# Own input places for the third recurrence pair, four places for the attention gates, and another K order in six output tiles

## What is computed

```python
proj = h @ w_in                        # a_q, a_k, a_v, a_z, g_q, g_f, g_i, g_z: 8 parts of 1024 columns
att  = chunk_attention(a_q, a_k, a_v)  # 8 heads of 128, softmax over a band, relative bias
att  = att * silu(a_z)                 # the attention gates
hg   = hgrn2(g_q, g_f, g_i)            # 8 heads: q = silu(g_q), decay from sigmoid(g_f), a recurrence in chunks of 64
hg   = rms(hg) * silu(g_z)
x    = x + gate * (concatenate([att, hg]) @ w_out)
```

## Time and profile before

| what | value |
|---|---|
| median of the runs | 1596.85 us |
| span of the profiled execution | 1599.0 us |
| TensorE busy | 1573.0 us (98%) |
| VectorE busy | 1154.1 us (72%) |
| ScalarE busy | 862.4 us (54%) |
| DMA | 331 MB, mean 207 GB/s |
| mean granted TensorE clock | 0.994 of full speed |

### The profile page before, as it was taken

The page is one execution under the profiler, slowest core; times in us unless marked ns, Lnnn a source line. Parts: engine busy times, 40 slices in busy tenths (PEclk is TensorE's granted clock), DMA queues, the critical chain, the costliest instruction groups (busy, mean ns, idle before and its releaser), DMA issues.

```text
span 1599.0 us, 24289 instructions
## 1 busy us (share of the span) xinstructions
PE 1573.0 (98%) x9650; PEld 1400.7 (88%) x9650; DVE 1154.1 (72%) x1696; ACT 862.4 (54%) x1321; POOL 151.6 (9%) x164
## 2 busy tenths in 40 slices
PE   8998999989999999999999999999999999999999
PEld 6787889988999999988799888888888888888887
DVE  6797867877778886759778777777777777455544
ACT  6855546767665555655556454544444444444442
POOL 0000000321221220034213000000000000000000
PEclk9999999999999999999999999999999999999999
DMA  9999975533457774343244545555455454555552
GB/s 373 369 343 349 365 285 209 188 114 121 180 189 267 285 272 179 132 158 132 97 144 178 189 170 199 184 186 210 172 197 191 179 211 175 205 199 185 198 196 105
DMA packets 47825, 331.02 MB, mean 207 GB/s; under 512 B 5281, under 2 KB 6689, under 8 KB 8417
## 3 DMA queue, kind: packets, MB, share of 16 engines
q1 hardware_dynamic: 45184, 312.20, 53.5%
q0 software_dynamic: 2240, 17.04, 2.8%
q10 hardware_dynamic: 290, 0.25, 0.1%
HBM read 327.37 MB, written 2.10 MB: 206 GB/s over the span
## 4 chain that ended last, share of the span: by engine, by line
PE 89%; DVE 5%; DMA 3%; ACT 2%; issue 1%; POOL 0%; SPq 0%; ACTq 0%; DVEq 0%; POOLq 0%
PE ps L1173 20%; PE ps L1174 11%; PE ps L1169 9%; PE ps L1170 8%; PE ps L1171 8%; PE ps L1228 5%; PE ps L1227 5%; PE ps L1226 5%; PE ps L1216 4%; PE ps L1217 3%; PE ps L1218 3%; DVE wl L1916 2%; DMA raw<-in_wts 1%; DMA xs<-in_xN 1%; PE ps L1384 1%; PE ps L1351 1%
## 5 line engine op out<-in xcount | busy, mean ns | idle before, releaser
L1916 DVE TENSOR_TENSOR wl<-raw,wh 128x1024 fp32r<-128x1024 f32 x512 | 626.2, 1236 | 282.4 <-ACT wh L1519 281.9
L1519 ACT ACTIVATE wh<-raw 128x1024 fp32r<-128x1024 f32 x512 | 531.3, 1054 | 377.2 <-PE ps L1228 130.6
L1173 PE MATMUL ps<-hA,wh 128*128 128x512 f32 x1408 | 488.7, 390 | 0.0
L1174 PE MATMUL ps<-hA,wl 128*128 128x256 f32 x1408 | 397.0, 282 | 0.0
L1173 PEld LDWEIGHTS ps<-hA,wh 128*128 128x128 f32 x1408 | 264.2, 188 | 55.3
L1174 PEld LDWEIGHTS ps<-hA,wl 128*128 128x128 f32 x1408 | 266.1, 189 | 0.0
L1169 PE MATMUL ps<-hA,wh 128*128 128x256 f32 x752 | 219.5, 292 | 0.0
L1170 PE MATMUL ps<-hA,wh 128*128 128x256 f32 x752 | 211.7, 282 | 0.0
L1171 PE MATMUL ps<-hA,wl 128*128 128x256 f32 x752 | 211.7, 282 | 0.0
L1169 PE MATMUL ps<-hB,wh 128*128 128x256 f32 x576 | 164.4, 285 | 0.8 <-DVE work L2362 0.4
L1170 PE MATMUL ps<-hB,wh 128*128 128x256 f32 x576 | 161.1, 280 | 0.0
(11 more groups left out here) (303 smaller groups left out, 2077.9 us busy)
## 6 DMA issues: line engine op xcount, KB each, us to landing
raw<-in_wts SPq DMA_DIRECT2D x256, 1024.0 KB, 4.8
raw<-in_ada SPq DMA_DIRECT2D x36, 1024.0 KB, 6.1
side<-in_ada POOLq DMA_DIRECT2D x12, 1024.0 KB, 8.5
work<-in_memN SPq DMA_DIRECT2D x2, 1024.0 KB, 8.9
xs<-in_xN POOLq DMA_DIRECT2D x1, 2048.0 KB, 20.6
xs<-in_xT POOLq DMA_DIRECT2D x2, 1024.0 KB, 7.8
out_rows<-xs SPq DMA_DIRECT2D x8, 256.0 KB, 2.4
wp<-in_dt SPq DMA_DIRECT2D x8, 128.0 KB, 2.7
```

What stands on the lines that cost most here:

```text
L1173: e.matmul(ps[bank][:, :], w1, hl, start=first, stop=False)
L1174: i = e.matmul(ps[bank][:, T:2 * T], w2, hl[:, 0:T], start=False, stop=last)
L1519: e.activation(wh[:, h % WS, :], raw[:, n % RAW, part * HALF:(part + 1) * HALF], ACT.Copy).then_inc(s_hi)
L1916: e.tensor_tensor(wl[:, h % WS, :], src, wh[:, h % WS, :].bitcast(F32), ALU.subtract).then_inc(s_lo)
```

## The change

1. A tensor `third` of three places lies over K steps 12 to 14 of the tensor `hB2`. By `INPUT_SET = (1, 0, 2, 1)` pair 0 has the second place of f, q, z, pair 1 the first, pair 2 the places in `third`, pair 3 pair 0's. The calls `until(rt 0)` and `until(rt 1)` ahead of the tiles of pairs 2 and 3 become one, `until(rt 0)` ahead of those of pair 3. The head of the recurrence `rf` p now itself waits for `rt` p-2 (a new generator `rec_head`, and a semaphore wait of ScalarE ahead of the sigmoids), as kk and E still have two places.
2. The four gate tiles have a place each: the three that pair 1 used and one in `av`. So az0 now stands behind `until(rt 1)`, az3 behind attention heads 0 to 3, and the waits for `gate` n-2 are gone.
3. The first six tiles of the output product take their K in another order. `until` for heads 4 to 7, for gates 2 and 3, and the load of x stand ahead of its fifth half instead of its first. `rt` 3 is still asked for ahead of block 64; K steps 14 and 15 still begin at block 66.

```diff
+INPUT_SET = (1, 0, 2, 1)
 OUT_FIRST = 6
-OUT_PARTS = (tuple(range(8, 14)), (0, 2, 4, 6, 7), (14, 15), (1, 3, 5))
+OUT_STEPS = ((range(0, 4), (8, 9, 10, 11)), (range(0, 4), (0, 2)), (range(0, 4), (12, 13)), (range(4, 6), (8, 9, 10, 11, 12, 13, 0, 2)),
+             (range(0, 6), (4, 6, 7)), (range(0, 6), (14, 15)), (range(0, 6), (1, 3, 5)))
+    def rec_head(p):
+        while p >= 2 and ("rt", p - 2) not in o.done:
+            yield
+        yield from stages(("rf", p), REC_HEAD)
...
-        if kind != "az" and n >= 2:
-            o.until(("rt", n - 2))
+        if kind != "az" and n == 3:
+            o.until(("rt", 0))
         if kind == "az":
             if n == 0:
+                o.until(("rt", 1))
+            if n == 3:
                 o.until(*[("att", h) for h in range(4)])
-            if n >= 2:
-                o.until(("gate", n - 2))
...
-    o.until(*[("att", h) for h in range(4, 8)])
-    o.beat("xload", 0)
...
-    o.until(*[("rt", n) for n in range(3)])
-    o.until(*[("gate", m) for m in range(4)])
-    for i, h in enumerate(OUT_PARTS[1]):
-        o.add(i % 2, ("gs", h), stages(("gs", h), ("hi", "lo")))
+    def split_gates(*heads):
+        for lane, h in heads:
+            o.add(lane, ("gs", h), stages(("gs", h), ("hi", "lo")))
+
+    o.until(("rt", 0), ("rt", 1))
     for i in range(0, 16 * OUT_FIRST, 8):
+        if i == 8:
+            o.until(("gate", 0), ("gate", 1))
+            split_gates((5, 0), (5, 2))
+        if i == 16:
+            o.until(("gs", 0), ("gs", 2))
+        if i == 24:
+            o.until(("rt", 2))
         if i == 32:
-            o.until(*[("gs", h) for h in OUT_PARTS[1]])
+            o.until(*[("att", h) for h in range(4, 8)])
+            o.beat("xload", 0)
+            o.until(("gate", 2), ("gate", 3))
+            split_gates((0, 4), (1, 6), (0, 7))
+        if i == 48:
+            o.until(("gs", 4), ("gs", 6), ("gs", 7))
         if i == 64:
             o.until(("rt", 3))
...
                 if k == "sigmoid":
                     e.wait_ge(*after(("f", 2 * pr + 1), "act", "ev"))
+                    if pr >= 2:
+                        e.wait_ge(*after(("rt", pr - 2), "dve", "lo"))
...
-        zt = [av[:, 0, i, :] for i in range(2)]
+        zt = [fin2[:, 0, :], qin2[:, 0, :], zin2[:, 0, :], av[:, 0, 0, :]]
```

More of the change, by code:

```diff
@@ L142, in plan @@
             ada(2, gates.pop(0))
-    early, ends, late, last = [], [], [], []
     for j in range(KT):
@@ L146, in plan @@
             ada(2, gates.pop(0))
-        t = s_tile("w_out", (128 * j,))
-        if j < OUT_FIRST:
-            early.append([t[kt] for kt in OUT_PARTS[0]])
-            ends.append([t[kt] for kt in OUT_PARTS[1]])
-            late.append([t[kt] for kt in OUT_PARTS[2]])
-            last.append([t[kt] for kt in OUT_PARTS[3]])
-        else:
+        if j >= OUT_FIRST:
+            t = s_tile("w_out", (128 * j,))
             out.append(("s", "w_out", t[8:] + t[:8]))
         if j == OUT_FIRST - 1:
-            line = [b for part in (early, ends, late, last) for t in part for b in t]
+            line = [("w_out", kt, (128 * i,)) for i, kt in OUT_LINE]
             out += [("s", "w_out", line[16 * i:16 * i + 16]) for i in range(OUT_FIRST)]
@@ L965, in program @@
         a1 = 0
-        fin, a1 = carve(a1, 2, 512, of=early)
-        qin, a1 = carve(a1, 2, 512, of=early)
-        zin, a1 = carve(a1, 2, 512, of=early)
+        fin2, a1 = carve(a1, 2, 512, of=early)
+        qin2, a1 = carve(a1, 2, 512, of=early)
+        zin2, a1 = carve(a1, 2, 512, of=early)
+        fin, zin, qin = ([(pair[:, 0, :], pair[:, 1, :], third[:, i, :])[n] for n in INPUT_SET] for i, pair in enumerate((fin2, zin2, qin2)))
         kk, a1 = carve(a1, 512, of=early)
@@ L1374, in rec_end @@
                     e.wait_ge(*after(t, "act", "sq"))
-                    e.matmul(ps[6][:, :], ones[:], fin[:, t[1] % 2, :], start=True, stop=True).then_inc(mark(t, "pe", "ss"))
+                    e.matmul(ps[6][:, :], ones[:], fin[t[1]], start=True, stop=True).then_inc(mark(t, "pe", "ss"))
             def softmax(t, k, bank, pairs, causal, v, B):
@@ L1709, in gate_split @@
                     e.wait_ge(*after(("gate", h // 2), "dve", "os"))
-                    e.wait_ge(*after(("rt", 3 if h in (1, 3, 5) else 2), "dve", "lo"))
+                    e.wait_ge(*after(("rt", 3 if h in (1, 3, 5) else 1 if h in (0, 2, 4) else 2), "dve", "lo"))
                     e.activation(hB2[:, h, 0:T], O(h), ACT.Copy).then_inc(mark(t, "act", "hi"))
```

44 lines of the change are left out of this document (21 added, 23 removed).

## The result

The changed kernel takes **1607.1 us** (median of 7 runs, 1602.8 to 1609.7) against 1597.8 us of the kernel before on the same chip: ratio 1.0051, 95% interval 1.0037 to 1.0065. It is slower by 0.5%, where 1588 us was forecast. That is rival C: the direction of the forecast was wrong, and 1607 lies outside its range. The profiled execution is the slowest of the seven: its time was 1609.7 us and its span, which leaves out some 2 us of the time in every profiled run here, 1607.9. (The 1599.0 us of the kernel before are a span too, so that execution lay some 4 us above the median, and not 2.15. The forecast took its difference off the median, so nothing in it hangs on this.)

A forecast was written before the change was run, and what follows sets the result against it. TensorE, busy 98% of the span, was taken as the bound, losing 13.8 us in two stretches. -13.8 + 1.6 + 0.5 + 0.5 + 0.5 + 1.7 = -9.0 us, so 1596.85 became 1588 us, range 1582 to 1596.

The forecast's parts named there:

- rival C: Slower: the four pairs' chain falls behind, TensorE waits at block 66 longer than it saved; 1603 to 1609, chance 0.07.
- The stretches and their price: Two `until` stretches ahead of f2 and f3, 31.1 us long, lose TensorE 13.8 us, upper end 15.0, which the change gives back.
- Spreading: Some 20 task steps, now each in its own gap among products, cost 0.09 us each; 1.6 us taken.
- The wait at f3: Remaining `until(rt 0)`: TensorE arrives after about 39 us, pair 0's chain needs 32 to 38; 0.5 us wait, range 0 to 3.
- The new waits at the gates' K steps: Heads 0 and 2 split in half 145, multiplied in half 146, while ScalarE empties gate tiles: 0.5 us, range 0 to 2.
- The chain against the output product: Pair 3's `lo` against TensorE's earlier arrival at block 66, 516 to 526 against 520.6: 1.7 us new wait, range 0 to 6.
- the point of 532.8: Deciding point for the slower outcome: pair 3's `lo` ending later than 529.35 + 3.4 = 532.8 us.
- B: The wait only moves to f3: `until(rt 0)` still forces part of the chain, 3 to 6 us; 1590.5 to 1593.5, chance 0.13.
- The gates' waits: Old waits for gates n-2, halves 128 to 143, stand where TensorE never paused; their removal gives nothing.
- the order by K: New K order of output tiles takes no work away; the replaced waits cost nothing before; 0.5 us cost, range 0 to 2.
- The table load: ScalarE's table loads take 1.28 us without drain; with the skill page's drain the sum would be some 2 us higher.

The follow-up runs named there:

- e4b: Changed kernel with one wait put back, `until(rt 0)` ahead of f2, none for rt 1 ahead of f3: 1596.78 us, ratio 0.9989 to the kernel before.
- e1: Kernel before with only the new K order of the first six output tiles; places and early waits stay old: 1601.38 us, ratio 1.0014.
- e11: Changed kernel with the early waits for rt 0, rt 1 and gate n-2 all put back; new places and K order stay: 1600.42 us, ratio 1.0013.
- e2: Changed kernel with the old K order and the old `until` calls ahead of half 144; the new places stay: 1609.72 us, ratio 1.0071.
- e18: Changed kernel with the planner's `LEAD` at 0 instead of -0.5 in this stage alone, so steps may go out sooner: 1612.5 us, ratio 1.0086.
- e17: Changed kernel with the planner's `BEHIND` at 4.5 instead of 2.5 in this stage alone, letting attention lanes run further behind: 1611.07 us, ratio 1.0081.
- e3: Changed kernel with the waits for rt 0 and rt 1 put back, but not those for gate n-2; new places stay: 1606.98 us, ratio 1.0053.

## Why the prediction was wrong

**The stretches and their price: right.** Both are gone, clock and busy share from 331 to 479 are as forecast, and no DMA or product wait stands near 490. That giving them back can be worth time when the chain allows it is suggested by e4b, which drops one of the two: the stage in its one trace is 3.8 us shorter than before, but its ratio of 0.9989 has an interval that holds 1. The 13.8 us of the sum couldn't be measured by themselves.

**Spreading: right.** The sum had up to 20 steps at 0.09 us and took 1.6 us. Measured is 1.7 us more in gaps that hold a task step or stand right behind one. Only 8 such gaps more were counted, though, and not 20: the size came out right in part by luck.

**The wait at f3: right in size, wrong in meaning.** I had TensorE at f3 39 us after 330.9 and 32 to 38 us of chain ahead of it; a stretch of 4.2 us with 1.4 us of idle time stands at 360.2. TensorE came there 29.5 us after half 104 began (330.63), not 39: eight halves are 23.0, so 6.6 us of task steps had been done on the way where the working had 16. The product of f3 began at 364.4, and not at 370 to 373. That was the first sign of undone work. And that the wait got small meant that nearly nothing was put out there at the forced pace; I priced only TensorE's loss of it, not the chain's.

**The new waits at the gates' K steps: 0.5 us forecast; the loss shows here, but its cause is the chain.** The first `hB` product was to come near 494 to 496 and came at 479.4. Only 12.2 us of the 27.0 could be saved time; the other 14.8 us are steps of tasks that had not been done yet. The text read "early arrival" as gain, and it should have been the warning: what TensorE hasn't done by then, it must do behind. I named `until` at block 66 as the one place where the chain is asked for. The new order has five more such places, ahead of halves 145, 146, 147, 148 and 150, and those ahead of halves 146, 147 and 148 forced 31.6 us in three stretches; of the 47.8 us from 479.4, 20.8 were lost. The places alone are harmless while the chain is in time (e1, e11), and without them the loss is as large (e2).

**The chain against the output product: the failed step.** The sum took 1.7 us of new wait, range 0 to 6, from it. The working had pairs 0 and 1 at 5 to 10 us more each, pair 2 at 17 us less, and the end at 516 to 526. Measured from the first step to `ss`: pair 0 57.5 us (before 46.3), pair 1 59.2 (43.9), pair 2 75.6 (68.7), pair 3 33.7, forced (51.4). Two terms failed. The first is that each spread pair cost 11 and 15 us, over the upper end. The second is larger. Pair 2's 19.2 us of waiting for z3 went, as forecast (1.3 us from its last pv to `ss`), but from its first step to that pv it took 74.3 us instead of 49.5, which is more than the wait had been. It began 25.8 us late (415.86 against 390.05), and 25.8 + 24.8 - 17.9 leaves its `ss` 32.7 us late instead of early. The chain's end at 541.0 is 15 us over the range's upper end, and the stage is 8.8 us longer instead of 9.0 shorter.

Why are levels slower among products? Before, pair 1's first to sixth level (346.1 to 366.5) came 4.1 us apart with no `until` in between (the stretch ended at the first of them); in the changed kernel (361.4 to 393.7) 6.5 us apart:

```profile
346.10:366.50 20.40, 20.08 (x169) 19.77 (x169) 19.31 (x44) 13.74 (x31) 8.30 (x8) 1.00 0.34 116
```

```profile
361.40:393.70 32.30, 30.88 (x260) 30.69 (x259) 27.06 (x46) 23.80 (x38) 14.47 (x11) 1.00 0.46 168
```

The first is the kernel before, the second the changed one. VectorE does the same number of instructions (44 and 46), in 19.3 and 27.1 us: four weight splits (L1916, 1.32 us each) in the first, nine (L1930, 1.31 us) in the second. The second window also holds a product for the output gate (L1976, 3.1 us) and the head of pair 2. So behind a stretch, in which the splits had run ahead of TensorE, the chain has VectorE more to itself. That is argued from counts, no run tests it, and it is half of an answer at most. VectorE isn't full in the second window (84%; 95% in the first) and e18 and e17, which let steps out sooner or with fuller engines, made some pairs quicker and others slower. **What sets the pace of a level among products stays open.** Not tried was a kernel that leaves the weight splits of this stage out.

**The rivals.** C was right in its outcome, its price (1603 to 1609) and, in the main, its mechanism, the chain of four pairs behind the point of 532.8. But TensorE did not wait at block 66, as C had it (1.5 us there); it waited ahead of halves 146 to 148. I looked for the loss at block 66 alone, and gave C a chance of 0.07 on the strength of "each pair some 5 us slower than the upper ends": the pairs that were spread were 1 to 5 us over them, and pair 2, whose gain I took as sure, did the rest. B's remark on the forced order was nearer: the wait moved, though not to f3.

**The gates' waits and the order by K.** "Their removal gives nothing" was true of TensorE's idle time and false of the chain: e3 against e11, 7 us. "It takes no work away, 0.5 us" for the order by K stands: e1, 1.0014 with an interval that holds 1.

**The table load.** Pair 2's sigmoids waited 0.59 us for rt 0's `lo`, within the 0 to 1 us given:

```profile
366.40 1.28 ACT L1625 ACT_TABLE_LOAD   x1 [0.59 <-DVE hB L2119]
367.69 0.63 ACT L1625 ACTIVATE early<-third 128x512 f32<-128x512 f32 x1
```

The activation starts 1.29 us after the load, as in the earlier trace rows. The 1.38 us of drain that the Trainium skill puts beside a table load (page "ScalarE: Activation LUTs", section "What ACT_TABLE_LOAD costs") don't show here either.

## What to carry to other kernels

In a kernel whose order is planned, a wait on the bounding engine may be doing work: it is the place where a long chain is driven forward. Before taking it away, find where the chain is asked for last, count what must be done by then, and read an early arrival of the busy engine as undone work until the step counts say otherwise. The cheapest repair here was one wait kept of several (e4b: 10 us against the changed kernel), though which one had to be tried (e3, with two, gave nothing). Before two traces are compared, check where the stage in question begins in each. And for each due point ahead of the end, "resume time + work left" shows which of them bounds, to 1 or 2 us.

## What the runs showed of the hardware

The granted clock followed the stretches to their new place. Five microseconds at the end of the second one:

```profile
505.00:510.00 5.00, 4.05 (x19) 4.08 (x20) 3.58 (x6) 0.63 (x1) 3.63 (x4) 0.50 0.00 0
```

19 matmuls at clock 0.50, that is 1.2 of 2.4 GHz, though a product had begun again at 505.95; until 509.9 its matmuls stand 0.21 us apart, at full clock 0.12. But a stretch need not lower the clock where it is emptiest: in e18, with 16 instructions in 5 us, it was 1.00:

```profile
520.00:525.00 5.00, 3.34 (x16) 2.03 (x14) 1.23 (x6) 2.34 (x7) 0.00 (x0) 1.00 0.00 0
```

In the 4 us behind that (525.0 to 529.0, 6 instructions) it was 0.86. So the drop can't be put down to a stretch by its length alone (15.4 us in e18 at a mean clock of 0.96, 15.4 us in e4b at 0.89), and it may come only with the product behind the stretch: in e18 TensorE had 11 instructions from 489.0 to 493.6 at clock 1.00, and from 494.0 to 500.0, full of product, 0.50.
